# The last product of a two-layer decoder trunk as seven half-size block products, with weight sums made by GpSimd

## The chip, the cores and the metric

The kernel runs on one core of a Trainium2 chip. The metric is the device time of one launch in microseconds (us). The core has TensorE (PE in the profile) for matrix products, VectorE (DVE) and ScalarE (ACT) for elementwise work, GpSimd (POOL) for more of it, and SyncE (SP), which here only starts DMA transfers. The engines run their own instruction lists in order and meet at semaphores.

## The reference, cut to what matters

The stream is 512 tokens by 1024 channels in float32, through two layers. Each layer is a mixer and then a SwiGLU block. The change is in the SwiGLU block of the second layer (l = 1) and in the final norm behind it; D_FF is 2816.

```python
h = rms_norm(x, ffn_norm_w[l])
x = x + (jax.nn.silu(h @ w_gate[l]) * (h @ w_up[l])) @ w_down[l]
...
return rms_norm(x, final_norm_w)
```

The product with `w_down[1]` is the "last product": 512 x 2816 times 2816 x 1024.

## The kernel before

**Precision.** Every large product is made of three TensorE matmuls on rounded float32 (fp32r) operands. A float32 tile W is split into a high part (a ScalarE copy into fp32r, `hi`) and a low part (a VectorE subtraction W - high, `lo`), and the same for the activations; `product` then issues high x high, high x low and low x high.

**The weight stream.** Weights come from HBM in 197 tiles of 128 x 1024 float32 (512 KB) by one DMA each, in SyncE's queue, into `raw`, which has RAW = 2 slots. A slot is loaded again when the split of the tile in it is done. The split goes into `wring`, RING = 4 slots of a high and a low part; ScalarE fills a slot when TensorE has used up the tile four places before (`tile_used`). So TensorE can have at most four split tiles ahead of it. The semaphores of this are `raw_loaded`, `hi_ready`, `lo_ready` and `tile_used`.

**The gate and up products** of layer 2 take 44 tiles, in loops on all engines. Each pair of tiles gives one 128-row block of the activations of the last product, in `AA` (22 blocks, each with a high and a low part of 512 tokens).

**The last product** takes 22 tiles, from T_DN1 on. `token_down(n, u, k)` multiplies token block n (128 of 512 tokens, the stationary operand) and the half u of weight tile k (512 columns, the moving operand) into PSUM bank 2n+u: 4 x 2 x 3 = 24 matmuls for a tile, 528 in all. The last four tiles are run bank by bank, so that the banks close one after another.

**The end.** For each token block VectorE adds the two banks to the residual `resid` (`final_sum`), ScalarE sums squares and takes a root, VectorE makes the reciprocal and the scaled output, and SyncE stores it. The last half block is scaled by ScalarE and stored from ScalarE's queue.

**Order.** All lists are written out by hand; no scheduler moves them. In the last product VectorE has one split per tile and nothing else, and GpSimd has no work at all. GpSimd works in the second layer's mixer alone, beside VectorE and beside the tile splits (`lo`, line 1091); that stage, at 670 to 800 us, is the place of this trace where both run elementwise instructions at once.

## Time and profile before

| | |
|---|---|
| Time before, median of 3 runs | 1249.27 us (1247.49 to 1369.76) |
| The profiled execution | span 1245.8 us from the first to the last instruction; it has no time of its own in the list, and its span is 3.5 us under the median |
| PE, DVE, ACT, POOL busy | 99%, 53%, 39%, 5% of the span |
| Chain that ended last | PE 91%, DVE 4%, ACT 3% |
| Last product on TensorE | 1119.7 to 1239.1 us |
| Granted TensorE clock | 0.999 on the mean |

The profile is of one execution. "Busy" counts the time in which an engine works on an instruction; for TensorE, whose matmuls overlap, it says little on how fast they follow each other, so the prediction counts matmuls in a window instead. The chain that ended last is followed back from the last instruction through whatever each step waited for. The wait rows name the engine and line that waited and what released it.

### The profile page before, as it was taken

The page shows a single profiled execution, that of the slowest core. Times are in us where ns is not written, and L with a number is a line of the kernel's source. Part 1 is how long each engine was busy: PE and PEld are TensorE (multiplying, and loading weights), DVE is VectorE, ACT ScalarE, POOL GpSimd, SP SyncE. Part 2 cuts the span into 40 slices and gives each one's busy share as a digit, 9 for nine tenths or more (in the row PEclk, how much of TensorE's full clock was granted, in tenths as well). Part 3 has the DMA queues.
Part 4 walks back from the last instruction along what each step waited for, and adds up shares of the span by engine and source line. Part 5 has one row for each costly group of instructions (what it writes and reads, how often), then busy time and mean ns, then how long its engine had stood idle before and what let it go on. Part 6 is the DMA issues. An engine that isn't in the chain of part 4 may idle for free.

```text
span 1245.8 us, 16247 instructions
## 1 busy us (share of the span) xinstructions
PE 1232.2 (99%) x5937; PEld 997.3 (80%) x5937; DVE 663.9 (53%) x1075; ACT 486.9 (39%) x802; POOL 65.6 (5%) x161
## 2 busy tenths in 40 slices
PE   9999999999999999999999999999999999999997
PEld 7876657888888888888888788888888888888886
DVE  6787876544444442226677666545644444442224
ACT  6344455433333322124575254544343333322123
POOL 0000000000000000000002814300000000000000
PEclk9999999999999999999999999999999999999999
DMA  7232412323222223222321201012254333223221
GB/s 246 102 112 74 119 38 68 102 102 101 100 91 90 89 101 118 95 90 68 119 85 68 85 35 51 35 51 73 87 145 114 109 101 106 92 101 118 94 93 67
DMA packets 50866, 116.33 MB, mean 93 GB/s; under 512 B 21250, under 2 KB 21506, under 8 KB 50818
## 3 DMA queue, kind: packets, MB, share of 16 engines
q1 hardware_dynamic: 49906, 114.33, 27.8%
q10 hardware_dynamic: 912, 1.35, 0.4%
q8 instruction: 31, 0.51, 0.2%
q14 instruction: 17, 0.14, 0.0%
HBM read 107.11 MB, written 2.10 MB: 88 GB/s over the span
## 4 chain that ended last, share of the span: by engine, by line
PE 91%; DVE 4%; ACT 3%; issue 1%; DMA 0%; ACTq 0%; SPq 0%; DVEq 0%
PE PS L1557 90%; PE PS L1633 0%; DMA raw<-w_stream 0%; DVE cacc L1236 0%; ACTq L793 0%; DVE resid L1532 0%; DVE outT L1548 0%; DVE wring L1091 0%; ACT unread L990 0%; DVE amax L1154 0%; PE PS L1856 0%; ACT wring L668 0%; DVE wbuf L1165 0%; DVE hbuf L1362 0%; ACT pbuf L752 0%
## 5 line engine op out<-in xcount | busy, mean ns | idle before, releaser
L1557 PE MATMUL PS<-HH,wring 128*128 128x512 f32 x3096 | 723.9, 392 | 0.9 <-DVE vd L1489 0.9
L1557 PEld LDWEIGHTS PS<-HH,wring 128*128 128x128 f32 x3096 | 575.4, 188 | 119.0 <-issue 1.3
L1557 PE MATMUL PS<-AA,wring 128*128 128x512 f32 (+1 forms) x792 | 183.3, 391 | 0.4 <-DVE AA L1170 0.3
L1557 PEld LDWEIGHTS PS<-AA,wring 128*128 128x128 f32 x792 | 148.1, 188 | 32.2 <-issue 1.0
L1062 DVE TENSOR_TENSOR ubuf<-PS,rstd 128x512 f32<-128x512 f32 x44 | 30.4, 691 | 191.4 <-PE PS L1557 191.4
L1084 DVE TENSOR_TENSOR wring<-raw,wring 128x1024 fp32r<-128x1024 f32 x36 | 44.1, 1226 | 147.4 <-ACT wring L724 147.4
L1557 PE MATMUL PS<-wring,AA 128*128 128x512 f32 x528 | 119.8, 389 | 0.0
L1557 PEld LDWEIGHTS PS<-wring,AA 128*128 128x128 f32 x528 | 99.1, 188 | 20.6
L1071 DVE TENSOR_TENSOR wring<-raw,wring 128x1024 fp32r<-128x1024 f32 x88 | 107.6, 1222 | 4.1 <-ACT wring L711 3.6
L668 ACT ACTIVATE wring<-raw 128x1024 fp32r<-128x1024 f32 x69 | 72.6, 1057 | 85.1 <-PE PS L1557 65.1
L1091 DVE TENSOR_TENSOR wring<-raw,wring 128x1024 fp32r<-128x1024 f32 x69 | 85.0, 1235 | 34.7 <-ACT wring L668 34.6
L706 ACT ACTIVATE AA<-ubuf 128x512 f32 x44 | 27.9, 633 | 192.1 <-DVE ubuf L1069 192.1
L724 ACT ACTIVATE wring<-raw 128x1024 fp32r<-128x1024 f32 x36 | 38.2, 1061 | 153.3 <-PE PS L1557 147.7
L711 ACT ACTIVATE wring<-raw 128x1024 fp32r<-128x1024 f32 x88 | 92.0, 1046 | 3.6 <-DMA raw<-w_stream 3.6
L700 ACT ACTIVATE gbuf<-gbuf 128x512 f32<-128x512 f32 x44 | 27.8, 632 | 117.1 <-DVE gbuf L1062 117.1
L1062 DVE TENSOR_TENSOR gbuf<-PS,rstd 128x512 f32<-128x512 f32 x44 | 30.4, 690 | 37.3 <-PE PS L1557 37.1
L1557 PE MATMUL PS<-wring,HH 128*128 128x512 f32 x192 | 45.8, 393 | 0.7 <-ACT wring L738 0.7
L1557 PEld LDWEIGHTS PS<-wring,HH 128*128 128x128 f32 x192 | 35.5, 188 | 8.5 <-issue 1.3
L752 ACT ACTIVATE pbuf<-PS,amax 128x128 f32<-128x128 f32 (+3 forms) x32 | 16.6, 524 | 47.6 <-DVE amax L1154 47.6
L1069 DVE TENSOR_TENSOR ubuf<-gbuf,ubuf 128x512 f32<-128x512 f32 x44 | 30.4, 692 | 5.8
L612 POOL MEMSET cin<- 128x3 f32 x1 | 0.1, 102 | 587.5 <-DVE xT L1052 587.5
L672 ACT ACTIVATE HH<-xT,vec 128x512 fp32r<-128x512 f32 x32 | 22.9, 716 | 20.0 <-DVE xT L1052 16.8
(282 smaller groups left out, 1043.4 us busy)
## 6 DMA issues: line engine op xcount, KB each, us to landing
raw<-w_stream SPq DMA_DIRECT2D x193, 512.0 KB, 3.3
reps<-ub SPq DMA_DIRECT2D x32, 66.5 KB, 2.1
resid<-turned SPq DMA_DIRECT2D x16, 128.0 KB, 4.9
out_t<-outT SPq DMA_DIRECT2D x3, 512.0 KB, 2.6
reps_b<-ub SPq DMA_DIRECT2D x16, 66.5 KB, 2.1
reps<-ub ACTq DMA_DIRECT2D x16, 66.5 KB, 2.4
xT<-x_t SPq DMA_DIRECT2D x4, 256.0 KB, 5.3
raw<-w_stream SPq DMA_DIRECT2D x4, 256.0 KB, 5.8
```

The costliest lines, as they stand in the source:

```text
L668: nc.scalar.activation(wring[:, t % RING, 0], raw_tile(t), ACT.Copy).then_inc(hi_ready[t % RING], 1)
L672: nc.scalar.activation(HH[:, n, 0], xT[:, n], ACT.Copy, scale=vcol(V_NORM + KD * s + n)).then_inc(feed_hi, 1)
L700: nc.scalar.activation(gbuf[:, c], gbuf[:, c], ACT.Silu).then_inc(sem("gate_silu"), 1)
L706: nc.scalar.activation(AA[:, bass.ds(r * 2 + c, 1), 0].rearrange("p a b -> p (a b)"), ubuf[:, c], ACT.Copy).then_inc(sem("ffn_hi"), 1)
L711: nc.scalar.activation(wring[:, t % RING, 0], raw[:, t % RAW], ACT.Copy).then_inc(hi_ready[t % RING], 1)
L724: nc.scalar.activation(wring[:, t % RING, 0], raw[:, t % RAW], ACT.Copy).then_inc(hi_ready[t % RING], 1)
L1062: V.tensor_tensor(buf[:, c], PS[:, 2 * c + u], rstd[:], ALU.mult).then_inc(evacuated, 1)
L1069: V.tensor_tensor(ubuf[:, c], gbuf[:, c], ubuf[:, c], ALU.mult).then_inc(sem("ffn_mul"), 1)
L1071: V.tensor_tensor(wring[:, t % RING, 1], raw[:, t % RAW], wring[:, t % RING, 0].bitcast(f32), ALU.subtract).then_inc(lo_ready[t % RING], 1)
L1084: V.tensor_tensor(wring[:, t % RING, 1], raw[:, t % RAW], wring[:, t % RING, 0].bitcast(f32), ALU.subtract).then_inc(lo_ready[t % RING], 1)
L1091: V.tensor_tensor(wring[:, t % RING, 1], raw_tile(t), wring[:, t % RING, 0].bitcast(f32), ALU.subtract).then_inc(lo_ready[t % RING], 1)
L1557: return nc.tensor.matmul(out, lhsT, rhs, start=start, stop=stop)
```

## The change

The last product is cut into a 2 x 2 scheme: tokens in halves (0 to 255 and 256 to 511), the 22 row blocks of the weights by parity (11 even, 11 odd), the columns in halves of 512. With A11, A12, A21, A22 for the activations (token half, parity) and B11, B12, B21, B22 for the weights (parity, column half), seven products of half the size in each of the three directions take the place of eight. The weights of the last product come from their own tensor `w_last`, block by block, in pieces of two rows of 128 x 512 (PIECES = 6 for one block: five of 1024 columns and one of 512). The code's products run in this order:

| product (pieces g) | activations | weights |
|---|---|---|
| P_12 (0 to 5) | A11 | B12, from the stream |
| P_11 (6 to 11) | A21 - A22 | B11, loaded into `kept` |
| P_22 (12 to 17) | A12 | B22, from the stream |
| P_21 (18 to 23) | A22 | B11 + B21, in `kept` |
| P_SUM (24 to 29) | A11 - A21 + A22 | B11 + B21 + B22, in `kept` |
| P_ALL (30 to 35) | A21 - A11 | B11 + B21 + B22 + B12, in `kept` |
| P_LAST (36 to 41) | A12 - A11 + A21 - A22 | B22, loaded into `kept` anew, + B21 |

- GpSimd adds an addend to each piece of `kept` in place, 24 additions (`add_to_kept`). The addends are loaded by SyncE into two slots (`addends`), and a slot is loaded again when its addition is done. An addition also waits until VectorE has split the piece's earlier value.
- Each of the 42 pieces is split as before by ScalarE (`last_hi`) and VectorE (`last_lo`), four pieces ahead of TensorE at most.
- The sums of activations are made by VectorE: two subtractions in each round of the gate/up loop, and pairs of instructions on 128 x 512 with a split behind them between the pieces (`last_product`), the splits' high parts by ScalarE.
- Two PSUM banks for each product; P_22, P_21 and P_LAST add onto banks that hold an earlier product. Behind a product, VectorE adds its banks to `resid` and to two snapshots (`after_product`).
- The loads of `kept` begin when the gate and up products are over, since they lie where HH was.
- The output order becomes token blocks 2, 3, 0, 1; the squares of half of the outputs are summed earlier. Elsewhere some semaphores are merged.

```diff
-N_TILES = T_DN1 + KF
+N_TILES = T_DN1
+HALF = KF // 2
+PIECES = (HALF + 1) // 2
+PRODUCTS = 7
...
+B11, B12, B21, B22 = (0, 0), (0, 1), (1, 0), (1, 1)
+P_12, P_11, P_22, P_21, P_SUM, P_ALL, P_LAST = range(PRODUCTS)
+OUT_ORDER = (2, 3, 0, 1)
+BANK_12, BANK_21, BANK_SUM, BANK_22 = 4, 6, 0, 2
+PRODUCT_BANK = (BANK_12, BANK_21, BANK_12, BANK_21, BANK_SUM, BANK_22, BANK_SUM)
+RING_PRODUCTS = (P_12, P_22)
+ADDED = (P_21, P_SUM, P_ALL, P_LAST)
+ADDENDS = 2
+ADDED_PARTS = {P_21: (B21, P_11), P_SUM: (B22, P_21), P_ALL: (B12, P_SUM), P_LAST: (B21, P_ALL)}
...
+    pfull, q = at("pfull", [HALF, 2 * P], f32, SCRATCH + 128)
+    assert q <= base
+    kept, q = at("kept", [HALF, S], f32, at_H)
+    addends, q = at("addends", [ADDENDS, TILE], f32, q)
+    assert q <= at_H + 32768
...
+        def ring_load(g, part):
+            v = ring_use(g)
+            before = ring_before(v - RAW)
+            sp.wait_ge(hi_ready[before % RING], slot_round(before))
+            sp.wait_ge(lo_ready[before % RING], slot_round(before))
+            n = len(piece_rows(g % PIECES)) * S
+            sp.dma_start(raw[:, v % RAW, 0:n], last_d[part][:, columns_of(g % PIECES)]).then_inc(raw_loaded[v % RAW], 16)
...
+        for i in range(PIECES):
+            ring_load(P_12 * PIECES + i, B12)
+        sp.wait_ge(tile_used, T_DN1)
+        for i in range(PIECES):
+            sp.dma_start(kept_tile(i), last_d[B11][:, columns_of(i)]).then_inc(kept_loaded[i], 16)
+        def load_addend(a, i):
+            d = ADDED.index(a) * PIECES + i
+            if d >= ADDENDS:
+                sp.wait_ge(added, d - ADDENDS + 1)
+            n = len(piece_rows(i)) * S
+            sp.dma_start(addends[:, d % ADDENDS, 0:n], last_d[ADDED_PARTS[a][0]][:, columns_of(i)]).then_inc(addend_loaded[d % ADDENDS], 16)
...
+        for i in range(PIECES):
+            if i == RAW:
+                for k in range(PIECES):
+                    load_addend(P_21, k)
+            ring_load(P_22 * PIECES + i, B22)
+        for a in (P_SUM, P_ALL):
+            for i in range(PIECES):
+                load_addend(a, i)
+        for i in range(PIECES):
+            free = last_tile(P_ALL * PIECES + i)
+            sp.wait_ge(lo_ready[free % RING], slot_round(free))
+            sp.dma_start(kept_tile(i), last_d[B22][:, columns_of(i)]).then_inc(kept_loaded[i], 16)
+            load_addend(P_LAST, i)
...
+        def add_to_kept(a, i):
+            d = ADDED.index(a) * PIECES + i
+            free = last_tile(ADDED_PARTS[a][1] * PIECES + i)
+            pool.wait_ge(lo_ready[free % RING], slot_round(free))
+            if a == P_LAST:
+                pool.wait_ge(kept_loaded[i], 48)
+            elif a > P_21:
+                pool.wait_ge(added, added_count(ADDED[ADDED.index(a) - 1], i))
+            pool.wait_ge(addend_loaded[d % ADDENDS], 16 * (d // ADDENDS + 1))
+            n = len(piece_rows(i)) * S
+            nc.gpsimd.tensor_tensor(kept_tile(i), kept_tile(i), addends[:, d % ADDENDS, 0:n], ALU.add).then_inc(added, 1)
...
+        for a in ADDED:
+            for i in range(PIECES):
+                add_to_kept(a, i)
...
+        def last_hi(g):
+            product, i = divmod(g, PIECES)
+            t = last_tile(g)
+            n = len(piece_rows(i)) * S
+            if product in RING_PRODUCTS:
+                v = ring_use(g)
+                act.wait_ge(raw_loaded[v % RAW], raw_count(v))
+                src = raw[:, v % RAW, 0:n]
+            else:
+                if product == P_11:
+                    act.wait_ge(kept_loaded[i], 32)
+                else:
+                    act.wait_ge(added, added_count(product, i))
+                src = kept_tile(i)
+            act.wait_ge(tile_used, t - RING + 1)
+            nc.scalar.activation(wring[:, t % RING, 0, 0:n], src, ACT.Copy).then_inc(hi_ready[t % RING], 1)
...
+                    V.tensor_tensor(ubuf[:, c], gbuf[:, c], ubuf[:, c], ALU.mult).then_inc(sem("ffn_mul"), 1)
+                    if c:
+                        dve.wait_ge(sem("ffn_mul"), r * 3 + (KF + 2))
+                        V.tensor_tensor(ubuf[:, 0, 2 * P:S], ubuf[:, 0, 2 * P:S], ubuf[:, 1, 2 * P:S], ALU.subtract).then_inc(sem("ffn_mul"), 1)
+                    loop_lo(r, tg + RING + 2 * c)
+                    if c:
+                        dve.wait_ge(sem("ffn_mul"), r * 3 + (KF + 3))
+                        V.tensor_tensor(pfull[:, bass.ds(r, 1)].rearrange("p a b -> p (a b)"), ubuf[:, 0, 0:2 * P], ubuf[:, 0, 2 * P:S],
+                                        ALU.subtract).then_inc(sem("lhs_made"), 1)
...
+        def last_lo(g):
+            product, i = divmod(g, PIECES)
+            t = last_tile(g)
+            n = len(piece_rows(i)) * S
+            src = raw[:, ring_use(g) % RAW, 0:n] if product in RING_PRODUCTS else kept_tile(i)
+            dve.wait_ge(hi_ready[t % RING], slot_round(t))
+            V.tensor_tensor(wring[:, t % RING, 1, 0:n], src, wring[:, t % RING, 0, 0:n].bitcast(f32), ALU.subtract).then_inc(lo_ready[t % RING], 1)
...
+        def after_product(product):
+            banks = [PS[:, PRODUCT_BANK[product] + b] for b in range(2)]
+            if product == P_11:
+                dve.wait_ge(sem("last_act"), 2)
+            for b in range(2):
+                product_done(dve, product, b)
+                if product == P_11:
+                    V.tensor_tensor(snap(b), banks[b], snap(b), ALU.add).then_inc(sem("last_sums"), 1)
+                elif product == P_22:
+                    dve.wait_ge(sem("last_sums"), sums_made(P_11, b))
+                    add_residual(b, 1, banks[b], ALU.add).then_inc(sem("final_x"), 1)
+                    link(add_residual(b, 0, snap(b), ALU.add))
+                    add_residual(b, 0, banks[b], ALU.subtract).then_inc(sem("last_sums"), 1)
...
+        def last_product():
+            dve.wait_ge(sem("lhs_made"), HALF)
+            dve.wait_ge(sem("resid_loaded"), 16 * 16)
+            for g in range(RING, PRODUCTS * PIECES):
+                last_lo(g)
+                if 5 <= g < 11:
+                    i = g - 5
+                    dve.wait_ge(sem("ffn_lo"), 2 * KF)
+                    link(V.tensor_tensor(scratch(i), second_more(i, 0).bitcast(f32), full_sum(i), ALU.subtract))
+                    V.tensor_tensor(scratch(i), scratch(i), second_more(i, 1).bitcast(f32), ALU.add).then_inc(sem("lhs_made"), 1)
+                if 6 <= g < 12:
+                    i = g - 6
+                    dve.wait_ge(sem("ffn_hi"), 2 * KF + i + 1)
+                    V.tensor_tensor(first_rows(i, 1), scratch(i), first_rows(i, 0).bitcast(f32), ALU.subtract).then_inc(sem("ffn_lo"), 1)
+                elif 12 <= g < 18:
+                    i = g - 12
+                    dve.wait_ge(sem("ffn_hi"), 2 * KF + PIECES + i + 1)
+                    V.tensor_tensor(first_diff(i, 1), full_sum(i), first_diff(i, 0).bitcast(f32), ALU.subtract).then_inc(sem("ffn_lo"), 1)
+                if 17 <= g < 29 and g % 2 == 1:
+                    i = (g - 17) // 2
+                    link(V.tensor_tensor(scratch(i), second_rows(i, 0).bitcast(f32), full_sum(i), ALU.subtract))
+                    V.tensor_tensor(scratch(i), scratch(i), second_rows(i, 1).bitcast(f32), ALU.add).then_inc(sem("lhs_made"), 1)
+                elif 18 <= g < 30:
+                    i = (g - 18) // 2
+                    dve.wait_ge(sem("ffn_hi"), 2 * KF + 2 * PIECES + i + 1)
+                    V.tensor_tensor(second_rows(i, 1), scratch(i), second_rows(i, 0).bitcast(f32), ALU.subtract).then_inc(sem("ffn_lo"), 1)
+                if g % PIECES == 4 and g // PIECES >= 2:
+                    after_product(g // PIECES - 1)
...
-        def token_down(n, u, k):
-            return product(PS[:, 2 * n + u], (AA[:, k, 0, blk(n)], AA[:, k, 1, blk(n)]), wpair((T_DN1 + k) % RING, slice(u * S, (u + 1) * S)),
-                           k == 0, k == KF - 1)
-        pe.wait_ge(norm_rstd, 4)
...
+        def left(product, r, b):
+            some = slice(b * P, (b + 1) * P)
+            more = slice((2 + b) * P, (3 + b) * P)
+            of = {P_12: (0, some), P_11: (0, more), P_22: (1, some), P_21: (1, more), P_SUM: (0, more), P_ALL: (0, some), P_LAST: (1, some)}[product]
+            return pairs_of[:, r, of[0], 0, of[1]], pairs_of[:, r, of[0], 1, of[1]]
...
+        def piece(a, i, b):
+            adds = a in (P_22, P_21, P_LAST)
+            t = last_tile(a * PIECES + i)
+            for m, r in enumerate(piece_rows(i)):
+                last = product(PS[:, PRODUCT_BANK[a] + b], left(a, r, b), wpair(t % RING, slice(m * S, (m + 1) * S)),
+                               r == 0 and not adds, r == HALF - 1, adds)
+            return last
+        for a in range(PRODUCTS):
+            bank_ready(a)
+            for i in range(PIECES if a < P_LAST else PIECES - RING):
+                arrived(last_tile(a * PIECES + i))
+                left_ready(a, i)
+                last = piece(a, i, 0)
+                if i == PIECES - 1:
+                    last.then_inc(last_mm, 1)
+                piece(a, i, 1).then_inc(tile_used, 1)
```

How the lists read before and after, at three places. The names: `wring` is the ring of split pieces, `raw` the slots of loads, `kept` and `addends` as above, `pfull` holds A11 - A21 + A22, `gbuf` and `ubuf` are scratch, `ssq` and `rstd` are the two snapshots.

VectorE in the last product, before: tiles 4 places ahead of TensorE, then the end.

```order
L1084 TENSOR_TENSOR wring<-raw,wring 128x1024 [waits hi_ready0]
L1084 TENSOR_TENSOR wring<-raw,wring 128x1024 [waits hi_ready1]
L1084 TENSOR_TENSOR wring<-raw,wring 128x1024 [waits hi_ready2]
L1080 REGISTER_ALU
L1080 COMPARE_AND_BRANCH
L1091 TENSOR_TENSOR wring<-raw,wring 128x1024 [waits hi_ready3]
L1091 TENSOR_TENSOR wring<-raw,wring 128x1024 [waits hi_ready0]
L1532 TENSOR_TENSOR resid<-resid,PS 128x512 [waits token_down,final_loaded,resid_loaded]
L1536 TENSOR_SCALAR nst<-ost 128x1 [waits final_sq]
L1532 TENSOR_TENSOR resid<-resid,PS 128x512 [waits token_down]
```

VectorE after, from the first split of product P_21 (g = 18) on.

```order
L1342 TENSOR_TENSOR wring<-kept,wring 128x1024 [waits hi_ready1]
L1399 TENSOR_TENSOR AA<-gbuf,AA 128x2x256 [waits ffn_hi]
L1342 TENSOR_TENSOR wring<-kept,wring 128x1024 [waits hi_ready2]
L1394 TENSOR_TENSOR gbuf<-AA,pfull 128x512
L1395 TENSOR_TENSOR gbuf<-gbuf,AA 128x512 [waits dve_chain]
L1342 TENSOR_TENSOR wring<-kept,wring 128x1024 [waits hi_ready3]
L1399 TENSOR_TENSOR AA<-gbuf,AA 128x2x256 [waits ffn_hi]
L1342 TENSOR_TENSOR wring<-kept,wring 128x1024 [waits hi_ready0]
L1394 TENSOR_TENSOR ubuf<-AA,pfull 128x512
L1395 TENSOR_TENSOR ubuf<-ubuf,AA 128x512 [waits dve_chain]
L1342 TENSOR_TENSOR wring<-kept,wring 128x1024 [waits hi_ready1]
L1399 TENSOR_TENSOR AA<-ubuf,AA 128x2x256 [waits ffn_hi]
```

Between two splits there now stand one or two instructions more for the activations' sums, whose inputs are all in SBUF as the splits' are; a split of `kept` waits for ScalarE, which waits for GpSimd.

GpSimd's list, before: its last rows, at the end of the mixer of layer 2.

```order
L650 TENSOR_TENSOR G_122<-G_122 128x4x2 [waits gdn1_pool]
L648 TENSOR_TENSOR G_122<-G_123,G_122 128x4 [waits gdn1_pool]
L650 TENSOR_TENSOR G_122<-G_122 128x4 [waits gdn1_pool]
L653 TENSOR_TENSOR G_123<-G_122,consts 128x512 [waits gdn1_pool]
L2107 UNCONDITIONAL_BRANCH
```

GpSimd after: from the fourth of the 24 additions on, which stand behind the same L653 row (now L788).

```order
L803 TENSOR_TENSOR kept<-kept,addends 128x1024 [waits addend_loaded1,lo_ready0]
L803 TENSOR_TENSOR kept<-kept,addends 128x1024 [waits addend_loaded0,lo_ready1]
L803 TENSOR_TENSOR kept<-kept,addends 128x512 [waits addend_loaded1,lo_ready2]
L803 TENSOR_TENSOR kept<-kept,addends 128x1024 [waits addend_loaded0,added,lo_ready1]
L803 TENSOR_TENSOR kept<-kept,addends 128x1024 [waits addend_loaded1,added,lo_ready2]
L803 TENSOR_TENSOR kept<-kept,addends 128x1024 [waits addend_loaded0,added,lo_ready3]
```

A list that had ended goes on with additions, each of which waits for a load and for a split by VectorE, and from the seventh on for an earlier addition.

TensorE at the end, before: the last full tile, and the four that are run bank by bank.

```order
L1557 MATMUL PS<-wring,AA 128x512 [waits ffn_lo,lo_ready0,hi_ready0]
L1557 MATMUL PS<-wring,AA 128x512 x23
L1557 MATMUL PS<-wring,AA 128x512 [waits lo_ready1,hi_ready1,ffn_lo]
L1557 MATMUL PS<-wring,AA 128x512 x5
L1557 MATMUL PS<-wring,AA 128x512 [waits lo_ready2,hi_ready2]
L1557 MATMUL PS<-wring,AA 128x512 x5
L1557 MATMUL PS<-wring,AA 128x512 [waits lo_ready3,hi_ready3]
L1557 MATMUL PS<-wring,AA 128x512 x5
L1557 MATMUL PS<-wring,AA 128x512 [waits lo_ready0,hi_ready0]
L1557 MATMUL PS<-wring,AA 128x512 x77
```

TensorE after: the start of P_LAST and the end.

```order
L1876 MATMUL PS<-wring,AA 128x512 [waits lo_ready3,ffn_lo,hi_ready3,last_sums]
L1876 MATMUL PS<-wring,AA 128x512 x11
L1876 MATMUL PS<-wring,AA 128x512 [waits ffn_lo,lo_ready0,hi_ready0]
L1876 MATMUL PS<-wring,AA 128x512 x11
L1876 MATMUL PS<-wring,AA 128x512 [waits ffn_lo,lo_ready1,hi_ready1]
L1876 MATMUL PS<-wring,AA 128x512 x5
L1876 MATMUL PS<-wring,AA 128x512 [waits ffn_lo,lo_ready2,hi_ready2]
L1876 MATMUL PS<-wring,AA 128x512 x5
L1876 MATMUL PS<-wring,AA 128x512 [waits ffn_lo,lo_ready3,hi_ready3]
L1876 MATMUL PS<-wring,AA 128x512 x5
L1876 MATMUL PS<-wring,AA 128x512 [waits ffn_lo,lo_ready0,hi_ready0]
L1876 MATMUL PS<-wring,AA 128x512 x23
```

A piece of 1024 columns is now 12 matmuls where a tile was 24, and every piece waits anew for its split; the last two banks close 21 matmuls apart (the 24 of the last row less 3 that still belong to the first bank), where two banks before were 12 apart.

## Rows read from the trace of the kernel before

**Rows 1.** The page: its first line, busy engines, chain that ended last.

```profile
span 1245.8 us, 16247 instructions
PE 1232.2 (99%) x5937; PEld 997.3 (80%) x5937; DVE 663.9 (53%) x1075; ACT 486.9 (39%) x802; POOL 65.6 (5%) x161
...
PE 91%; DVE 4%; ACT 3%; issue 1%; DMA 0%; ACTq 0%; SPq 0%; DVEq 0%
```

**Rows 2.** Stretches: times, busy and instructions of PE, PEld, DVE, ACT, POOL; clock, DMA.

```profile
1120.00:1160.00 40.00, 40.00 (x178) 33.12 (x177) 12.34 (x12) 9.01 (x9) 0.00 (x0) 1.00 0.30 106
1119.70:1239.10 119.40, 119.35 (x527) 98.50 (x525) 35.58 (x42) 27.50 (x37) 0.00 (x0) 1.00 0.25 89
```

**Rows 3.** Waits from 1120 us on: who for whom, total, times, longest.

```profile
DVE wring L1084 <- ACT wring L724: 65.3, 16, 4.2
ACT wring L724 <- PE PS L1557: 65.2, 15, 4.4
...
SPq L580 <- DVE wring L1084: 78.6, 16, 5.0
```

**Rows 4.** Groups of the page: shapes, count, busy us, mean ns, idle before.

```profile
L1084 DVE TENSOR_TENSOR wring<-raw,wring 128x1024 fp32r<-128x1024 f32 x36 | 44.1, 1226 | 147.4 <-ACT wring L724 147.4
...
L724 ACT ACTIVATE wring<-raw 128x1024 fp32r<-128x1024 f32 x36 | 38.2, 1061 | 153.3 <-PE PS L1557 147.7
...
L1069 DVE TENSOR_TENSOR ubuf<-gbuf,ubuf 128x512 f32<-128x512 f32 x44 | 30.4, 692 | 5.8
```

**Rows 5.** Timeline, GpSimd with little beside it: start us, us, what.

```profile
776.66 1.29 POOL L633 TENSOR_TENSOR G<-G,consts 128x512 f32<-128x512 f32 x1 [8.21 <-DVE kT L1421]
...
778.03 0.74 POOL L635 TENSOR_TENSOR G<-G 128x256 f32<-128x256 f32 x1
...
778.84 0.47 POOL L637 TENSOR_TENSOR G<-G 128x128 f32<-128x128 f32 x1
```

**Rows 6.** Timeline, VectorE and GpSimd at once.

```profile
675.75 1.55 POOL L627 TENSOR_TENSOR vtok<-vtok,beta 128x512 f32<-128x512 f32 x1
676.33 0.68 DVE L1407 TENSOR_TENSOR G<-kT,PS 128x512 f32<-128x512 f32 x1
...
686.52 1.25 DVE L1091 TENSOR_TENSOR wring<-raw,wring 128x1024 fp32r<-128x1024 f32 x1
686.68 2.25 POOL L633 TENSOR_TENSOR G<-G,consts 128x512 f32<-128x512 f32 x1
689.01 0.74 POOL L635 TENSOR_TENSOR G<-G 128x256 f32<-128x256 f32 x1
689.05 1.78 DVE L1091 TENSOR_TENSOR wring<-raw,wring 128x1024 fp32r<-128x1024 f32 x1 [1.28 <-ACT wring L668]
...
701.05 1.23 DVE L1091 TENSOR_TENSOR wring<-raw,wring 128x1024 fp32r<-128x1024 f32 x1 [0.46 <-ACT wring L668]
701.26 1.09 POOL L650 TENSOR_TENSOR G<-G 128x16 f32<-128x16 f32 x1
702.44 0.21 POOL L648 TENSOR_TENSOR G<-G 128x12 f32<-128x12 f32 x1
```

**Rows 7.** DMA: issues from 1120 us (KB, median us to landing); stretch at the start.

```profile
raw<-w_stream SPq DMA_DIRECT2D x18, 512.0 KB, 3.2
...
12.00:16.00 4.00, 4.00 (x19) 3.33 (x18) 3.90 (x6) 3.84 (x7) 0.00 (x0) 1.00 1.03 410
```

**Rows 8.** Timeline as the last product begins.

```profile
1119.21 8.10 PE L1557 MATMUL PS<-wring,AA 128*128 128x512 f32 x35
1119.41 0.69 DVE L1062 TENSOR_TENSOR ubuf<-PS,rstd 128x512 f32<-128x512 f32 x1 [4.75 <-PE PS L1557]
...
1122.68 1.23 DVE L1071 TENSOR_TENSOR wring<-raw,wring 128x1024 fp32r<-128x1024 f32 x1
```

**Rows 9.** One-microsecond stretches behind the last matmul, columns as in rows 2.

```profile
1243.00:1244.00 1.00, 0.00 (x0) 0.00 (x0) 0.00 (x0) 0.00 (x0) 0.00 (x0) 0.72 0.45 168
1244.00:1245.00 1.00, 0.00 (x0) 0.00 (x0) 0.00 (x0) 0.00 (x0) 0.00 (x0) 0.50 0.95 356
```

379 lines of the change are left out of this document (246 added, 133 removed).

## The prediction

> **What bounds the kernel now.** I read the page first: TensorE is busy 99% of the span and holds 91% of the chain that ended last [rows 1]. Busy time of overlapping matmuls doesn't give their pace, so the next view is the stretches: 40 us inside the last product hold 178 matmuls, 0.2247 us each, and the whole product, 1119.7 to 1239.1, has 527 recorded of its 528 [rows 2]; 528 x 0.2247 = 118.6 us. The waits then show who is late: VectorE waits for ScalarE, ScalarE for TensorE, SyncE for VectorE's split, each some 65 to 79 us of these 119 [rows 3]. So TensorE alone sets the pace, and VectorE with 36 us and ScalarE with 27 us of work [rows 2] have much to spare. GpSimd does nothing there. The question is whether that stays so when TensorE's work shrinks and everybody else's grows.
>
> **TensorE's part, certain.** Seven products x 11 row blocks x 2 banks x 3 = 462 matmuls of the same shape, 66 fewer: 66 x 0.2247 = 14.8 us less. A product is 66 x 0.2247 = 14.8 us, a full piece (12 matmuls) 2.70 us, all seven 103.8 us.
>
> **What the others get.** Durations: a split of 1024 columns 1.23 us on VectorE and 1.06 on ScalarE; a VectorE instruction on 512 columns with both inputs in SBUF 0.69 [rows 4], which gives 0.42 for 256. GpSimd's additions on 1024 columns are in no row. Two-input instructions with little beside them took 0.47 for 128 columns, 0.74 for 256 and 1.29 for 512 [rows 5]: a straight line of 2.14 ns a column over 0.19 us, so 2.38 us for 1024 and 1.29 for the half piece. The 512-column row has a broadcast second input, and the line is stretched to twice its length, so I keep 2.2 and 2.6 as ends and take 2.38, since three rows lie on the line. A product's six additions take 5 x 2.38 + 1.29 = 13.2 us. By itself that fits under 14.8.
>
> The Trainium skill (GPSIMD Engine Reference, § 3.1 Elementwise — side-by-side cycle accounting) gives 4497 ns for an addition of 2048 columns; an estimate from it would be 2.25 us for 1024 and take about 2 us off the forecast. No row here has that width, and I go by the line.
>
> **The term that decides: VectorE and GpSimd don't overlap.** The timeline shows it [rows 6], in both directions. GpSimd's L633, 1.29 alone, started at 686.68 during a split and took 2.25: the split ended at 687.77, and the addition 1.16 later. The split that started at 689.05 while GpSimd's L635 ran until 689.75 took 1.78 instead of 1.23, ending 1.08 after it. A GpSimd instruction of 16 columns, 0.21 like its neighbour, took 1.09 beside a split. But VectorE's L1407, with one input in PSUM, took its usual 0.68 within GpSimd's 1.55. So VectorE instructions with two SBUF inputs and GpSimd's additions run one after the other, each for its duration less some 0.13 us of start: 1.10, 0.56 and 0.29 us for VectorE's three sizes, 2.26 and 1.17 for GpSimd's. I call this held time.
>
> The Trainium skill (SBUF — State Buffer, § Who interferes with whom) states this as an exclusive lock, for VectorE instructions with two SBUF inputs against GpSimd reads; it is the rule that speaks against this change. The trace agrees, with the rows just read. If it held only for some forms, the first rival below would be the result.
>
> All splits and all sums of activations have two SBUF inputs. Held time by product, from the list of the change (the splits of a product are always 5 x 1.10 + 0.56 = 6.1):
> - P_11: splits 6.1, sums 13 x 0.56 + 3 x 0.29 = 8.2, together 14.2; the first six additions, 5 x 2.26 + 1.17 = 12.5, fall here too.
> - P_22: splits 6.1, sums 7 x 0.56 + 0.29 = 4.2; no additions, since the next need the splits of P_21.
> - P_21: splits 6.1, sums 9 x 0.56 = 5.0, two snapshots onto `resid` 1.1, additions 12.5: 24.7.
> - P_SUM: splits 6.1, sums 4 x 0.56 + 4 x 0.29 = 3.4, snapshots 1.1, additions 12.5: 23.1.
> - P_ALL and P_LAST: splits 6.1 each, one set of additions, 12.5.
>
> TensorE offers 14.8 for each. Now in time, from TensorE's first matmul of the last product as zero.
>
> *P_12 and P_11.* The end of the gate/up loop keeps VectorE busy for 4 us past zero [rows 8], and the two new subtractions of 256 columns add 0.9: the last split of the loop ends near 5. Then SyncE loads piece 5 and the pieces of `kept`. A 512 KB transfer lands in 3.2 us, of which some 1.3 is transfer when several stand in line (410 GB/s) [rows 7]. `kept` 0 lands near 9.6, and its split starts near 11, when TensorE wants it at 14.8: no loss yet, but most of the lead of four pieces is gone. The addends stand behind eight transfers and GpSimd starts near 20. From 11 on the port is held 14.2 + 12.5 and 1.1 for the first split of P_22: P_22 can't start before 39, against 29.7. That is 9 late at least; I take 10.
> *P_22.* Its held time fits, but with two slots a pair of pieces takes a load, a copy and a split, 3.2 + 1.06 + 1.23 = 5.5, against TensorE's 5.4, so no lead is won back, and the first splits come with waits: 2 late, 0 at least.
> *P_21.* 24.7 - 14.8 = 9.9 late at least. Every split waits for ScalarE's copy (1.06), which VectorE can't fill, and the four PSUM instructions of `after_product` (4 x 0.68) leave the port idle behind the addition that runs with them: 2 more, 12.
> *P_SUM.* 23.1 - 14.8 = 8.3 at least, 10.5 likely, for the same reason.
> *P_ALL and P_LAST.* Held time over both is 12.2 + 12.5 = 24.7, under 29.6; P_ALL finds its sums made. P_LAST's need a new load of `kept` first: 1.5 late.
>
> Sum: 10 + 2 + 12 + 10.5 + 0 + 1.5 = 36 us late, less 14.8: **21 us slower**. At least: 9 + 0 + 9.9 + 8.3 = 27 late, +12. At most within this mechanism: no saving of the 0.13 us at the hand-overs, some 60 instructions in the three bound stretches, 8 us more, +29.
>
> **Edits at nothing.** The loop's new waits and subtractions cost VectorE 0.9 us per round of 21.6 us (96 matmuls), in which it works some 11; cover is the ring. The banks' waits (`last_act`, `last_sums`) are met a product ahead. The end: the last chain (residual, square, root, reciprocal, scaling, store) has the same instructions, and the other last bank closes 21 matmuls, 4.7 us, ahead, which covers its block's 3.5; within 0.5 us. More traffic, some 22 MB in 140 us, is 160 GB/s against the 410 of [rows 7]. The merged semaphores lie beside matmuls.
>
> **Time.** The profiled execution has a span of 1245.8 us, 3.5 under the median; the change is taken against both alike. 1249.3 + 21 = about **1271 us**. A measurement of this kernel can tell about 2%, 25 us, from no change.
>
> **Rivals.**
> *No block for these forms* (GpSimd's addition in place with plain inputs, VectorE's splits of `kept`). Then all fits under TensorE: 103.8, plus about 5: GpSimd begins at 20, SyncE's third piece of P_22 stands behind four of its additions and arrives near 36 where 35 is wanted, and the splits of P_21 and P_SUM follow with 1 to 2 us each. 118.6 - 108.8 = 10 less, 1240 us. This is the case on the faster side, though within 2%: 14.8 is all there is to win. For it: nothing but that no row shows a 1024-column addition. Against it: [rows 6]. Chance 0.14, with partial blocking in it (1235 to 1255).
> *TensorE's clock falls in its new gaps.* After the last matmul the granted clock was 0.72 in the fifth microsecond and 0.50 in the sixth [rows 9], 1.2 GHz. I expect gaps of 1 to 4 us between pieces, the longest at the ends of P_11, P_21 and P_SUM, some 45% of the time in P_21. At half clock a product takes 29.7, over the 26.8 and 25.3 that the port allows: 2.9 + 4.4, and 2 or so after P_11: 1280 us. It decides for slower by over 2% (above 1274.3). Against it: gaps between pieces are shorter than the idle time that the row shows. Chance 0.17 (1278 to 1290).
> The Trainium skill (TensorE: Matmul & The Clock Gate, § HAM oscillation — how this bites in real kernels) says that idle gaps between bursts of matmuls return the array to half clock; by it this rival would be the result, and [rows 9] agree only on the fall after the end.
> *The change doesn't do what it says:* excluded for the matmuls, which the order shows.
> *Worse than all this* (transfers late as well, GpSimd over 2.6 us): 0.06, above 1290.
>
> **The numbers.** Forecast 0.63, over 1261 to 1279, a quarter of it above 1274.3. Range 1250 to 1288: it leaves out most of the no-block case, the end of the clock case and the worst, 0.2. Slower by over 2%: 0.17 + 0.06 + 0.16 = 0.39; within 2%: 0.60; faster by over 2%: 0.01, since 14.8 us is 1.2%.
>
> **What will show it.** Additions of 1024 columns at 2.4 us where VectorE is idle and 3 to 3.5 beside it; splits of 1.2 us stretched to 2 to 3.5. TensorE dense until the end of P_11, then a matmul share near 55% in P_21 and P_SUM, waiting for splits; dense again in P_ALL. TensorE's last product 140 us long. If additions and splits overlap at their own durations, the step on held time is wrong; if `kept` or addends land late and GpSimd waits for DMA, the one on transfers is.

## The result and the profile after

The changed kernel takes 1272.49 us (median of 4 runs, 1270.81 to 1273.22), the kernel before 1248.42 us on the same chip. The ratio is 1.0196, with a 95% interval of 1.0182 to 1.0210: 24 us slower, where 21 to 22 were forecast (1271). The 1248.42 is the median of four runs, one of which, 1369.76 us, the ratio leaves out; the median of the other three is 1247.57 us.

The page of the profiled execution after: first line, busy engines, the 40 slices of three engines and of the clock, and the chain that ended last. It answers to [rows 1].

```profile
span 1271.1 us, 16397 instructions
...
PE 1229.4 (97%) x5871; PEld 989.1 (78%) x5871; DVE 762.8 (60%) x1172; ACT 515.9 (41%) x844; POOL 126.5 (10%) x185
...
PE   9999999999999999999999999999999999997677
...
DVE  6787876544444442227777566446654454578997
...
POOL 0000000000000000000006535000000000004544
PEclk9999999999999999999999999999999999998999
...
PE 84%; DVE 9%; ACT 3%; issue 2%; DMA 2%; ACTq 0%; POOL 0%; SPq 0%; DVEq 0%; POOLq 0%
```

TensorE has 66 matmuls fewer and 2.8 us less busy time, yet the span is 25.3 us longer: in the last four slices, where POOL shows 4 and 5, those of PE fall from 9 to 6 and 7. On the chain, PE fell from 91% to 84% and DVE rose from 4% to 9%.

TensorE's timeline in the last product (start, us, what; in brackets the idle time ahead and who ended it):

```profile
1120.96 15.35 PE L1876 MATMUL PS<-wring,AA 128*128 128x512 f32 x67
...
1152.71 4.32 PE L1876 MATMUL PS<-wring,AA 128*128 128x512 f32 x12 [5.75 <-DVE wring L1342]
1159.07 14.29 PE L1876 MATMUL PS<-wring,AA 128*128 128x512 f32 x54 [2.04 <-DVE wring L1342]
...
1179.10 2.97 PE L1876 MATMUL PS<-wring,AA 128*128 128x512 f32 x12 [1.06 <-DVE wring L1342]
1183.05 3.01 PE L1876 MATMUL PS<-wring,AA 128*128 128x512 f32 x12 [0.97 <-DVE wring L1342]
1187.59 3.01 PE L1876 MATMUL PS<-wring,AA 128*128 128x512 f32 x12 [1.54 <-DVE wring L1342]
...
1202.76 2.41 PE L1876 MATMUL PS<-wring,AA 128*128 128x512 f32 x6 [3.66 <-DVE wring L1342]
1206.29 7.51 PE L1876 MATMUL PS<-wring,AA 128*128 128x512 f32 x24 [1.12 <-DVE wring L1342]
...
1231.52 23.50 PE L1876 MATMUL PS<-wring,AA 128*128 128x512 f32 x102 [0.95 <-issue]
...
1257.43 5.71 PE L1876 MATMUL PS<-wring,AA 128*128 128x512 f32 x24 [0.17 <-issue]
```

The last product runs from 1120.96 to 1263.14, 142.2 us, against 119.84 before (1119.21 to 1239.05; it starts in [rows 8]). It is dense for P_12 and the first four of P_11's six pieces, waits 5.75 and 2.04 us ahead of the last two, has a gap ahead of nearly every piece of P_21 and P_SUM, and is dense again from P_ALL (1231.52) on. "Issue" in brackets does not mean that nothing was waited for: the weight load, which stands ahead of the matmul, took the wait for the split.

The stretches P_11, P_21 and P_SUM, columns as in [rows 2]:

```profile
1135.90:1161.60 25.70, 17.91 (x67) 13.83 (x66) 25.56 (x20) 9.58 (x14) 15.38 (x6) 0.88 0.46 163
1179.10:1206.30 27.20, 17.41 (x67) 12.32 (x67) 27.03 (x22) 8.72 (x14) 15.72 (x7) 0.95 0.33 93
1206.30:1231.50 25.20, 18.08 (x66) 13.34 (x67) 25.06 (x21) 9.75 (x15) 14.58 (x6) 0.92 0.29 88
```

VectorE, 36 us busy in the old last product [rows 2], is busy in 99% of each of these. GpSimd has spare time in all three. What VectorE does with its time is in the groups of the stretch 1119 to 1263 us (shapes, count, busy us, mean ns, idle before; the first row is GpSimd's):

```profile
L803 POOL TENSOR_TENSOR kept<-kept,addends 128x1024 f32<-128x1024 f32 x20 | 54.5, 2726 | 387.9 <-DMA addends<-w_last 354.9 <-DVE wring L1342 33.0
L1342 DVE TENSOR_TENSOR wring<-kept,wring 128x1024 fp32r<-128x1024 f32 x25 | 49.6, 1993 | 3.2 <-ACT wring L907 3.1
...
L1346 DVE TENSOR_TENSOR resid<-resid,PS 128x512 f32<-128x512 f32 x13 | 8.5, 680 | 0.1
...
L1382 DVE TENSOR_TENSOR gbuf<-AA,pfull 128x256 f32<-128x256 f32 x1 | 2.6, 2577 | 0.0
```

Splits of 1024 columns take 1993 ns on the mean, against 1226 in [rows 4]; one subtraction of 256 columns takes 2577 ns, where the prediction has 0.42 us for that width. The form with one input in PSUM (`resid<-resid,PS`) takes 680 ns, as before. And so it looks in time, in P_21:

```profile
1179.04 2.78 POOL L803 TENSOR_TENSOR kept<-kept,addends 128x1024 f32<-128x1024 f32 x1 [18.64 <-DVE wring L1342]
...
1179.48 3.42 DVE L1342 TENSOR_TENSOR wring<-kept,wring 128x1024 fp32r<-128x1024 f32 x1
...
1182.82 0.68 DVE L1394 TENSOR_TENSOR gbuf<-AA,pfull 128x512 f32<-128x512 f32 x1
1182.98 2.79 POOL L803 TENSOR_TENSOR kept<-kept,addends 128x1024 f32<-128x1024 f32 x1 [1.16 <-DVE wring L1342]
...
1183.53 2.78 DVE L1395 TENSOR_TENSOR gbuf<-gbuf,AA 128x512 f32<-128x512 f32 x1
```

The split begins 0.44 us after the addition and ends 1.08 after it (1182.90 against 1181.82). The next addition begins during VectorE's L1394 and ends 2.27 after it; L1395, behind it, ends 0.54 after that. These are the turns of the prediction, 2.26, 1.10 and 0.56 us: each instruction starts its own work when the other engine's has ended.

**The sum, read off the starts.** P_12, P_11, P_22, P_21, P_SUM and P_ALL start at 0, 15.0, 40.6, 58.1, 85.3 and 110.6 us after TensorE's first matmul, and P_LAST ends at 142.2.

| stretch | late, predicted | late, measured |
|---|---|---|
| to the start of P_22 | 10 | 10.7 |
| P_22 | 2 | 2.5 |
| P_21 | 12 | 12.2 |
| P_SUM | 10.5 | 10.3 |
| P_ALL and P_LAST | 1.5 | 1.7 |
| matmuls saved | -14.8 | -15.0 |
| last product | +21 | +22.3 |

"Late" is what lies over 14.96 us a product (66 x 0.2267: the 119.45 us from the first to the last matmul's start before, divided by 527 steps). The span's other 3 us: the last product starts 1.75 us later, and what follows the last matmul takes 8.0 instead of 6.75 us.

### The profile page after: what moved, and what is told of

It reads as the page before. It is cut to its first block, busy times and chain, and to the rows that moved or that the text cites. A ratio compares the mean times of both kernels' runs of the same rounds, so it can differ in the third digit from the quotient of the medians.

```text
span 1271.1 us, 16397 instructions
## 1 busy us (share of the span) xinstructions
PE 1229.4 (97%) x5871; PEld 989.1 (78%) x5871; DVE 762.8 (60%) x1172; ACT 515.9 (41%) x844; POOL 126.5 (10%) x185
## 4 chain that ended last, share of the span: by engine, by line
PE 84%; DVE 9%; ACT 3%; issue 2%; DMA 2%; ACTq 0%; POOL 0%; SPq 0%; DVEq 0%; POOLq 0%
PE PS L1876 83%; DVE wring L1342 2%; DMA raw<-w_last 1%; DVE resid L1346 1%; DVE gbuf L1382 1%; PE PS L1952 1%; DVE AA L1387 0%; DVE cacc L1550 0%; POOL kept L803 0%; ACTq L1015 0%; DVE gbuf L1383 0%; ACT wring L907 0%; DVE ubuf L1395 0%; DVE wring L1405 0%; DMA raw<-w_stream 0%
## 5 line engine op out<-in xcount | busy, mean ns | idle before, releaser
L1278 DVE TENSOR_TENSOR wring<-raw,wring 128x1024 fp32r<-128x1024 f32 x108 | 131.0, 1221 | 84.7 <-ACT wring L848 84.5
L848 ACT ACTIVATE wring<-raw 128x1024 fp32r<-128x1024 f32 x108 | 113.3, 1049 | 115.9 <-PE PS L1876 107.3
L1876 PE MATMUL PS<-wring,AA 128*128 128x512 f32 x462 | 115.3, 407 | 26.9 <-DVE wring L1342 19.0
L1876 PEld LDWEIGHTS PS<-wring,AA 128*128 128x128 f32 x462 | 89.0, 196 | 53.0 <-issue 34.9
L820 ACT ACTIVATE wring<-raw 128x1024 fp32r<-128x1024 f32 x67 | 70.5, 1057 | 77.0 <-PE PS L1876 56.8
L803 POOL TENSOR_TENSOR kept<-kept,addends 128x1024 f32<-128x1024 f32 (+1 forms) x24 | 61.2, 2553 | 396.9 <-DMA addends<-w_last 354.9
L1405 DVE TENSOR_TENSOR wring<-raw,wring 128x1024 fp32r<-128x1024 f32 x67 | 82.5, 1234 | 25.9 <-ACT wring L820 25.8
L1342 DVE TENSOR_TENSOR wring<-kept,wring 128x1024 fp32r<-128x1024 f32 (+1 forms) x30 | 54.0, 1808 | 3.2 <-ACT wring L907 3.1
L907 ACT ACTIVATE wring<-kept 128x1024 fp32r<-128x1024 f32 (+1 forms) x30 | 28.8, 978 | 16.9 <-PE PS L1876 8.4
```

The costliest lines, as they stand in the source:

```text
L803: nc.gpsimd.tensor_tensor(kept_tile(i), kept_tile(i), addends[:, d % ADDENDS, 0:n], ALU.add).then_inc(added, 1)
L820: nc.scalar.activation(wring[:, t % RING, 0], raw_tile(t), ACT.Copy).then_inc(hi_ready[t % RING], 1)
L848: nc.scalar.activation(wring[:, t % RING, 0], raw[:, t % RAW], ACT.Copy).then_inc(hi_ready[t % RING], 1)
L907: nc.scalar.activation(wring[:, t % RING, 0, 0:n], src, ACT.Copy).then_inc(hi_ready[t % RING], 1)
L1278: V.tensor_tensor(wring[:, t % RING, 1], raw[:, t % RAW], wring[:, t % RING, 0].bitcast(f32), ALU.subtract).then_inc(lo_ready[t % RING], 1)
L1342: V.tensor_tensor(wring[:, t % RING, 1, 0:n], src, wring[:, t % RING, 0, 0:n].bitcast(f32), ALU.subtract).then_inc(lo_ready[t % RING], 1)
```

## The experiments

Theory 1 is the prediction's: GpSimd's additions and VectorE's instructions with two inputs in SBUF take turns, and VectorE, which feeds TensorE, has no time for it in P_11, P_21 and P_SUM. Rival 2: not the turns, but the chain load, addition, split and the late addends. Rival 3: TensorE's clock. All edits are to the changed kernel, unless said otherwise, and are compared with its 1272.49 us above; "of before" is the kernel before beside the same runs (1247.69 to 1247.82 us). The first four (8 columns, memsets, half the columns, less work for VectorE) leave out part of the sums and are there for the time alone. "Last product" is its length on TensorE.

### Additions on 8 columns

```diff
-            nc.gpsimd.tensor_tensor(kept_tile(i), kept_tile(i), addends[:, d % ADDENDS, 0:n], ALU.add).then_inc(added, 1)
+            nc.gpsimd.tensor_tensor(kept_tile(i)[:, 0:8], kept_tile(i)[:, 0:8], addends[:, d % ADDENDS, 0:8], ALU.add).then_inc(added, 1)
```

> The changed kernel with each of the 24 weight additions of GpSimd on 8 of its 1024 (512) columns; every wait, load and semaphore stays, so the sums of the weights are left out. Theory 1 (GpSimd's additions and VectorE's subtractions with two inputs in SBUF hold each other up, and that is the whole loss): with the additions near 0.2 us nothing is left to block, the last product takes 105 us of matmuls and the first waits of the loads, 107 to 112 us, and the time is 1238 to 1243 us. Rival 2 (the loss is the chain: addends load only when an addition is done, and a piece's split waits for its sum): at least half of the 22 us stays, 1255 to 1270 us. Rival 3 (half clock in the gaps carries the loss): since the gaps go with the additions, it gives the same as theory 1 here and is told apart by the run with filled gaps.

1234.96 us, 0.9894 of before (0.9874 to 0.9914): 37.5 us less than the changed kernel, and 13 of the 15 us under the kernel before that 66 matmuls fewer allow. That is 3 us below the 1238 to 1243 expected. With every load, wait and semaphore in place the last product took 108.2 us, within the 107 to 112 expected; what follows the last matmul took 5.7 us instead of the changed kernel's 8.0, and the last product began at 1119.36 instead of 1120.96. Its timeline on TensorE:

```profile
1119.36 35.52 PE L1876 MATMUL PS<-wring,AA 128*128 128x512 f32 x156
1155.19 5.70 PE L1876 MATMUL PS<-wring,AA 128*128 128x512 f32 x24 [0.30 <-DVE wring L1342]
1161.21 4.33 PE L1876 MATMUL PS<-wring,AA 128*128 128x512 f32 x18 [0.32 <-DVE wring L1342]
1166.41 15.24 PE L1876 MATMUL PS<-wring,AA 128*128 128x512 f32 x66 [0.87 <-DVE wring L1342]
1182.46 45.12 PE L1876 MATMUL PS<-wring,AA 128*128 128x512 f32 x198 [0.81 <-DVE wring L1342]
```

Over the matmuls' 105 us (462 x 0.2267, and the last one's length) some 3 us are left: the 0.30 and 0.32 us stand in P_22, whose pieces are loaded, the 0.87 and 0.81 us at the starts of P_21 and P_SUM, where VectorE had worked without a pause since 1159.84. The rest of the loss hangs on the additions' width. That excludes the loads, but a tiny addition also answers some 2 us sooner, so it doesn't yet tell turns from latency.

### GpSimd as busy, but only writing

```diff
-            nc.gpsimd.tensor_tensor(kept_tile(i), kept_tile(i), addends[:, d % ADDENDS, 0:n], ALU.add).then_inc(added, 1)
+            nc.gpsimd.memset(addends[:, d % ADDENDS, 0:n], 0.001).then_inc(sem("warm_zero"), 1)
+            pool.wait_ge(sem("warm_zero"), d + 2)
+            nc.gpsimd.memset(kept_tile(i), 0.001).then_inc(added, 1)
```

> The changed kernel with two memsets (one of the addend slot, one of the kept piece) in place of each addition, so the sums of the weights are left out: GpSimd is busy about as long as with the addition (some 2.1 against 2.4 us for 1024 columns) and answers as late, but reads no SBUF. Theory 1, in the form that it is GpSimd's reads that stand against VectorE's: VectorE's splits of kept pieces stay near 1.3 us against 1.99 after, and the time is 1238 to 1246 us. Rival 2 (it is GpSimd's late answer, however it comes about): 1258 to 1270 us with splits near 1.3 us. A third way, writes contend as reads do: splits near 2 us and 1262 to 1272 us.

1239.54 us (two runs, 1237.49 and 1241.60; the profile is of the latter), 0.9931 of before (0.9908 to 0.9953). The last product took 111.7 us. The groups of this run:

```profile
L1344 DVE TENSOR_TENSOR wring<-kept,wring 128x1024 fp32r<-128x1024 f32 x25 | 30.5, 1222 | 11.2 <-ACT wring L909 11.0
...
L805 POOL MEMSET kept<- 128x1024 f32 x20 | 19.1, 957 | 1.1
L803 POOL MEMSET addends<- 128x1024 f32 x20 | 19.1, 956 | 383.3 <-DMA addends<-w_last 369.4 <-DVE wring L1344 13.8
```

A pair of memsets takes 2.0 us from start to end where an addition alone takes 2.4 (2.7 on the mean in the changed kernel), and the splits are at their own 1222 ns. Rival 2 expected 1258 or more. An answer nearly as late as the addition's costs 4.6 us over the run with 8 columns, for an answer 1.4 us later (there the additions took 0.57 us on the mean). At that price the 0.4 to 0.8 us by which the pair is still shorter than an addition are worth 1 to 3 us (an estimate). The other 30 of the 33 us up to the changed kernel are the reads' turns, which is theory 1.

The Trainium skill (SBUF — State Buffer, § Who interferes with whom) names a GpSimd instruction that reads SBUF as the other side, and not one that only writes it. The trace agrees: 1222 ns beside memsets, 1993 beside additions.

### Additions on half the columns

```diff
-            nc.gpsimd.tensor_tensor(kept_tile(i), kept_tile(i), addends[:, d % ADDENDS, 0:n], ALU.add).then_inc(added, 1)
+            nc.gpsimd.tensor_tensor(kept_tile(i)[:, 0:n // 2], kept_tile(i)[:, 0:n // 2], addends[:, d % ADDENDS, 0:n // 2], ALU.add).then_inc(added, 1)
```

> The changed kernel with each GpSimd addition on half of its columns (512 of 1024, 256 of 512), so the sums of the weights are left out in the other half. Theory 1: an addition then holds VectorE up for 1.17 instead of 2.26 us, additions and splits of a piece fit into the 2.72 us of its matmuls, and only the pieces at the end of P_11 and in P_21, where VectorE has its own sums too, are late: 5 to 14 us remain over the 105 of the matmuls, and the time is 1243 to 1254 us. In proportion to the width (rival: each us of GpSimd costs the same): 1254 us, half way between 1235 and 1272.5.

1250.03 us (1248.37 to 1253.16; the profile is of the slowest run), within theory 1's 1243 to 1254. The last product took 122.7 us: the first half of the width costs 14.5 us in it (from 108.2) and the second 19.5. A straight line between the two ends would give 125.2. That the second half costs more fits theory 1, where additions cost nothing until VectorE's spare time is used up. But the distance, 2.5 us, is small, and the run tells little between the two forms.

### Less work for VectorE, additions whole

```diff
-link(V.tensor_tensor(scratch(i), second_more(i, 0).bitcast(f32), full_sum(i), ALU.subtract))
-V.tensor_tensor(scratch(i), scratch(i), second_more(i, 1).bitcast(f32), ALU.add)
+link(V.tensor_tensor(scratch(i)[:, :, 0:8], second_more(i, 0)[:, :, 0:8].bitcast(f32), full_sum(i)[:, :, 0:8], ALU.subtract))
+V.tensor_tensor(scratch(i)[:, :, 0:8], scratch(i)[:, :, 0:8], second_more(i, 1)[:, :, 0:8].bitcast(f32), ALU.add)
```

and the same for `second_rows`.

> The changed kernel with the 22 VectorE subtractions and additions that make the left factors of P_SUM and P_LAST from the halves (two per piece, in the loops of 5 <= g < 11 and 17 <= g < 29) on 8 columns of each row; the weight additions stay whole, so the products of the two left sums are left out. Theory 1: what GpSimd blocks is VectorE's queue, so work taken off VectorE (some 13 us of duration, and the turns that it would wait for) gives back its share: 8 to 16 us less in the last product, 1256 to 1265 us. If the additions on GpSimd alone paced the pieces, at one per 2.4 to 2.8 us: no more than 3 us, 1269 to 1273 us.

1260.46 us (1259.93 and 1260.99), where theory 1 had 1256 to 1265 and a pace set by GpSimd 1269 or more. The last product took 130.8 us, 11.3 less than in the changed kernel. Three of the groups:

```profile
L803 POOL TENSOR_TENSOR kept<-kept,addends 128x1024 f32<-128x1024 f32 x20 | 54.4, 2727 | 376.6 <-DMA addends<-w_last 353.2 <-DVE wring L1342 23.4
...
L1395 DVE TENSOR_TENSOR gbuf<-gbuf,AA 128x8 f32<-128x8 f32 x1 | 2.4, 2378 | 0.0
...
L1394 DVE TENSOR_TENSOR gbuf<-AA,pfull 128x16 f32<-128x16 f32 x3 | 0.5, 163 | 0.0
```

The 24 instructions (the expectation says 22; it is four for each of six pieces) come to 20 x 0.69 + 4 x 0.42 = 15.5 us by their own lengths at full width and to some 24 x 0.17 = 4.1 now, 11.4 less. They were not that short in the trace: six of them still waited out an addition, as the one on 8 columns that took 2378 ns, and all 24 were busy 16.1 us, against 31.1 in the changed kernel. An addition costs its turn whatever VectorE has next, but the work taken off VectorE came back whole in the last product (11.4 and 11.3 us), while GpSimd's additions took as long as ever. So the limit is VectorE's queue, with the additions in it as if they were its own, and not the pace of GpSimd.

### The additions on VectorE

```diff
+        def add_to_kept(a, i):
+            d = ADDED.index(a) * PIECES + i
+            if a == P_LAST:
+                dve.wait_ge(kept_loaded[i], 48)
+            dve.wait_ge(addend_loaded[d % ADDENDS], 16 * (d // ADDENDS + 1))
+            n = len(piece_rows(i)) * S
+            V.tensor_tensor(kept_tile(i), kept_tile(i), addends[:, d % ADDENDS, 0:n], ALU.add).then_inc(added, 1)
...
                 last_lo(g)
+                for ahead in (4, 3):
+                    if P_21 * PIECES <= g + ahead and (ahead == 3) == (g + ahead >= P_LAST * PIECES) and g + ahead < PRODUCTS * PIECES:
+                        add_to_kept(*divmod(g + ahead, PIECES))
...
         for i in range(PIECES):
-            if i == RAW:
-                for k in range(PIECES):
-                    load_addend(P_21, k)
             ring_load(P_22 * PIECES + i, B22)
+            for k in ((), (0, 1), (), (2,), (3,), (4, 5))[i]:
+                load_addend(P_21, k)
```

> The same 24 additions, each by VectorE four pieces ahead of its use (three for the last product), GpSimd idle, and the P_21 addends loaded between the P_22 pieces on SyncE's queue. VectorE's busy time rises by 24 x 1.15 = 28 us, and none of its instructions is stretched. Theory 1: TensorE waits some 15 us for VectorE in P_22 to P_SUM, where additions, splits and activation sums come to more than the product's 15 us; the last product takes 118 to 125 us, and the time is 1247 to 1256 us, against 1272.5 with GpSimd and 1248.4 before. If the additions cost the same wherever they run (chain or loads): 1265 to 1275 us.

1254.33 us (1253.68 to 1255.51), 1.0051 of before (1.0035 to 1.0068), within the 1247 to 1256 expected. The stretch from the first wait in P_22 to P_ALL, columns as in [rows 2]:

```profile
1163.00:1210.00 47.00, 40.23 (x144) 30.30 (x144) 46.65 (x60) 18.78 (x29) 0.00 (x0) 0.85 0.46 135
```

and the group of the additions:

```profile
L1362 DVE TENSOR_TENSOR kept<-kept,addends 128x1024 f32<-128x1024 f32 x20 | 24.4, 1220 | 3.1 <-DMA addends<-w_last 3.1
```

An addition on VectorE takes 1.22 us of VectorE; on GpSimd it takes 2.26 us of VectorE. Taking all of them back is 18 us faster. But VectorE is still full here (46.65 of 47 us), the last product takes 124.5 us, and the change still doesn't pay. The clock is 0.85 in this stretch; what part of the 20 us over the matmuls' 105 is the clock's wasn't taken apart.

### The gaps filled, to keep the clock

```diff
+                spin({10: 38, 11: 12, 23: 24, 29: 22}.get(a * PIECES + i, 0))
                 arrived(last_tile(a * PIECES + i))
...
+        def spin(n):
+            if n:
+                pe.wait_ge(evacuated, E_GU1 + 2 * KF)
+            for _ in range(n):
+                mm(PS[:, BANK_22, 0:2 * P], pairs_of[:, 0, 1, 0, 2 * P:3 * P], pairs_of[:, 0, 1, 0, 2 * P:S])
```

> The changed kernel with 38, 12, 24 and 22 extra matmuls of 256 columns into a free PSUM bank ahead of the pieces 10, 11, 23 and 29, where TensorE idles 5.75, 2.04, 3.66 and 3.39 us, to keep its clock up. Rival 3 (the clock carries the loss): the pieces behind go at full clock (4.32 us of twelve matmuls back to 2.7, 7.51 us of 24 back to 5.5), and the time falls by 4 to 8 us, to 1264 to 1268 us. Theory 1: the pieces go faster but then wait for the same splits, and the time falls by 0 to 3 us, 1269.5 to 1273 us.

1272.67 us (1271.94 to 1273.64), against 1272.49 for the changed kernel: no change, where the rival had 1264 to 1268. The clock had fallen in the changed kernel. Two stretches of it, columns as in [rows 2], the granted clock third from the right:

```profile
1152.00:1156.00 4.00, 3.29 (x9) 2.67 (x10) 3.96 (x4) 0.44 (x2) 3.61 (x2) 0.57 0.50 138
...
1203.00:1211.00 8.00, 6.88 (x19) 4.98 (x19) 7.93 (x7) 2.53 (x3) 5.07 (x3) 0.57 0.34 91
```

and with the gaps filled:

```profile
1151.60:1154.60 3.00, 2.96 (x14) 2.50 (x15) 2.96 (x3) 0.09 (x1) 2.54 (x2) 1.00 0.47 158
...
1203.00:1211.00 8.00, 6.07 (x20) 4.81 (x20) 7.96 (x6) 2.53 (x3) 5.07 (x3) 0.79 0.44 131
```

The piece behind the longest gap, 4.32 us for twelve matmuls after, took 2.99 here at full clock. It gave nothing back, since the next piece still waited 1.97 us for its split: P_ALL began 110.45 us after the first matmul, against 110.56 in the changed kernel. The second place was mended only in part (0.79, 24 matmuls in 7.32 us, against 7.51). At full clock 24 matmuls take 5.71, as at 1257.43 in the changed kernel, so 1.8 us are at stake there. The next piece waited 0.80 us for its split after them all the same, and VectorE was busy 7.93 of those 8.00 us, which speaks for this fall being free too. The run shows it of the first fall only.

Behind P_ALL this run had a wait of 2.38 us in P_LAST that the changed kernel did not have; GpSimd had waited 2.92 and 1.38 us there for addends to land. Its last product was 145.2 us long for that, its start 1.2 us earlier and its end 1.4 us shorter than in the changed kernel. So the equal times alone would not show that the clock is free; the equal starts of P_ALL do.

### The kernel before, with additions beside it

```diff
+        pool.wait_ge(tile_used, T_DN1)
+        for m in range(2):
+            nc.gpsimd.memset(unused[:, m], 0.001).then_inc(sem("warm_zero"), 1)
+            pool.wait_ge(sem("warm_zero"), m + 2)
+        for k in range(KF - RING):
+            pool.wait_ge(tile_used, T_DN1 + max(k - 1, 0))
+            nc.gpsimd.tensor_tensor(unused[:, 0], unused[:, 0], unused[:, 1], ALU.add).then_inc(sem("warm_zero"), 1)
+            pool.wait_ge(sem("warm_zero"), k + 4)
```

> The kernel before, with 18 additions of 1024 columns on GpSimd, kept = kept + addend on unused SBUF that nothing else reads, one released by each finished weight tile of the last product. Theory 1, in the form that the blocking costs time only where VectorE has none to spare: VectorE is busy 1.23 us of each 5.4 us there, its splits beside an addition stretch from 1.23 to up to 3.4 us, TensorE waits for none, and the time stays at 1247 to 1250 us. If additions on GpSimd slow the kernel by themselves (SBUF traffic, TensorE's reads): 18 x some tenths of a us, 1252 us or more.

1247.70 us, 1.0001 of before (0.9990 to 1.0011), within the 1247 to 1250 expected. One round in the timeline:

```profile
1141.38 2.40 POOL L664 TENSOR_TENSOR unused<-unused 128x1024 f32<-128x1024 f32 x1 [3.04 <-PE PS L1567]
1142.37 2.50 DVE L1094 TENSOR_TENSOR wring<-raw,wring 128x1024 fp32r<-128x1024 f32 x1 [2.94 <-ACT wring L734]
```

and the groups of TensorE and of the splits:

```profile
L1567 PE MATMUL PS<-wring,AA 128*128 128x512 f32 x528 | 119.8, 389 | 0.0
...
L1094 DVE TENSOR_TENSOR wring<-raw,wring 128x1024 fp32r<-128x1024 f32 x16 | 40.8, 2550 | 41.1 <-ACT wring L734 41.1
```

Here nothing depends on the additions. The splits take 2550 ns on the mean, twice their length, and the one shown ends 1.09 us after the addition (1144.87 against 1143.78), as the pair at 689 us in [rows 6] does (1.08); the splits take 21 us more in all, and TensorE waits for none of it. The turns are there without any chain between the two engines, and cost nothing where VectorE has time.

### The additions by DMA

```diff
-            pool.wait_ge(addend_loaded[d % ADDENDS], 16 * (d // ADDENDS + 1))
-            n = len(piece_rows(i)) * S
-            nc.gpsimd.tensor_tensor(kept_tile(i), kept_tile(i), addends[:, d % ADDENDS, 0:n], ALU.add).then_inc(added, 1)
+            nc.gpsimd.dma_start(kept_tile(i), last_d[ADDED_PARTS[a][0]][:, columns_of(i)], accum_op=ALU.add).then_inc(accumulated[d % 3], 16)
```

with a wait for the transfer three places before, and ScalarE's copies waiting for `accumulated`; the loads of addends are gone.

> The whole product, with each weight sum made by the DMA: an accumulating transfer from DRAM onto the kept piece, issued on GpSimd's queue in place of the addition; no addend slots, no addition on any engine. Theory 1: nothing holds up VectorE, and the time is that of the run with tiny additions, 1234 to 1242 us, below the kernel before. Against it: an accumulating transfer reads and writes SBUF beside the DRAM and takes longer than the 3.6 us of a plain one; at 6 pieces of lead (15 us of a product) it is hidden up to some 10 us. If its transfer takes longer than that, or its descriptors cost GpSimd and the queues over 2.7 us a piece: 1250 us or more.

1243.41 us (1242.20 to 1245.04), 0.9965 of before (0.9951 to 0.9979). The splits took 1221 ns. The issues, from the DMA view (KB, median us to landing):

```profile
kept<-w_last POOLq DMA_DIRECT2D x20, 512.0 KB, 7.6
raw<-w_last SPq DMA_DIRECT2D x10, 512.0 KB, 4.0
kept<-w_last SPq DMA_DIRECT2D x10, 512.0 KB, 6.7
```

and the two longest waits in TensorE's timeline:

```profile
1156.50 5.72 PE L1868 MATMUL PS<-wring,AA 128*128 128x512 f32 x24 [2.23 <-DVE wring L1334]
...
1215.83 10.04 PE L1868 MATMUL PS<-wring,AA 128*128 128x512 f32 x36 [1.95 <-DVE wring L1334]
```

It missed its expectation (1234 to 1242) by 1.4 us, and the last product took 114.9 us. An accumulating transfer takes 7.6 us from issue to landing, a plain one of the same size 4.0 or 6.7, some of it standing in line with others. Ahead of the first wait ScalarE had waited 6.02 us for a plain load, whose slot comes free late; ahead of the second, 8.16 us for a piece of P_LAST, which is loaded and then added to. One more kernel gave both places more lead: pieces 0 and 1 of P_22 load into the two free addend slots, and P_LAST adds B21 where P_22 left pieces 0, 1, 4 and 5 of B22.

```diff
-            nc.gpsimd.dma_start(kept_tile(i), last_d[ADDED_PARTS[a][0]][:, columns_of(i)], accum_op=ALU.add)
+            nc.gpsimd.dma_start(last_source(a, i), last_d[ADDED_PARTS[a][0]][:, columns_of(i)], accum_op=ALU.add)
...
+        for i in range(2):
+            sp.dma_start(addends[:, i], last_d[B22][:, columns_of(i)]).then_inc(first_loaded[i], 16)
+        for i in range(2, PIECES):
+            ring_load(P_22 * PIECES + i, B22)
```

> The run with DMA additions (1243.4 us), with its two longest waits of TensorE taken away: 2.23 us ahead of the third piece of P_22, whose load waits for a slot, and 1.95 us ahead of P_LAST, whose pieces are loaded and then added to in turn. The pieces 0 and 1 of P_22 load into the two free addend slots as soon as the last product begins, and P_LAST adds B21 onto the pieces 0, 1, 4 and 5 of B22 where P_22 left them; only the pieces 2 and 3 are loaded again. Theory 1 with the DMA's lead as the only rest: 3 to 6 us less (the waits and the half clock behind the second, 36 matmuls in 10.04 us against 8.2), 1237 to 1241 us. If the waits are those of the accumulating transfers in general (7.6 us from issue to landing), they turn up at the next piece: 1242 to 1245 us.

1239.59 us (1238.77 to 1240.24), 0.9933 of before (0.9919 to 0.9947), within the 1237 to 1241 expected: the fastest kernel that computes the whole result, 8 us under the one before and 33 under the changed one. The last product took 110.6 us. The first wait is gone; in place of the second there are two, 1.45 and 1.39 us, further into P_LAST:

```profile
1119.29 45.06 PE L1878 MATMUL PS<-wring,AA 128*128 128x512 f32 x198
1165.10 15.25 PE L1878 MATMUL PS<-wring,AA 128*128 128x512 f32 x66 [0.75 <-DVE wring L1344]
...
1218.21 1.63 PE L1878 MATMUL PS<-wring,AA 128*128 128x512 f32 x6 [1.45 <-issue]
1221.22 8.62 PE L1878 MATMUL PS<-wring,AA 128*128 128x512 f32 x36 [1.39 <-issue]
```

## Why the prediction was right

**The term that decides** held. VectorE's two-input instructions and GpSimd's additions take turns, with the turn lengths that were read off [rows 6]. In P_21 two pieces have two additions, two splits and three sums: 2 x 2.26 + 2 x 1.10 + 3 x 0.56 = 8.4 us; TensorE's pieces there start 8.49 apart (1179.10 to 1187.59). The runs with 8 columns, with memsets and with less VectorE work each take away one side. What they leave to other causes (the loads, VectorE's own work and the late answer) is 7 us together: 111.7 us with memsets, less the matmuls' 105.

**The addition's length**, 2.38 off a line through three narrower rows, was 2.37 to 2.42 where VectorE left it alone (1149.10: 2.37, and 2.40 in the old kernel with additions). The estimate of 2.25 from the Trainium skill's table (GPSIMD Engine Reference, § 3.1 Elementwise — side-by-side cycle accounting) was 6% short of that. Beside VectorE the additions took 2.73 on the mean and 2.79 in P_21, less than the 3 to 3.5 named as a sign: there an addition stood behind the end of an earlier VectorE instruction only, and it was VectorE's own that were stretched.

**The lateness by product** was right to 0.7 us each, as the table shows. The places were right too: P_11's end, all of P_21 and P_SUM, nearly dense from P_ALL on (its longest gap there is 0.62 us). GpSimd's first addition came 21.1 us after TensorE's first matmul, where 20 stood.

**Sizes that were off, all small.** The pace, 0.2247 us, was read from a count in a window that takes in matmuls cut by both of its edges; from first to last it is 0.2267, 1 us more for 528. "The end ... within 0.5 us" was 1.2 us: VectorE's last residual add began 2.3 us after the last matmul, since `after_product(P_ALL)` and the scaled outputs of two blocks stood ahead of it; before, it began 1.2 us after. The later start of the last product, 1.75 us, was in no term. It goes with a granted clock of 0.83 at 800 to 810 us, far ahead of the change:

```profile
800.00:810.00 10.00, 10.00 (x69) 9.56 (x68) 3.51 (x6) 4.99 (x9) 0.00 (x0) 0.83 0.14 40
```

The profiled runs with half-width additions and with memsets have the same 0.83 and start at 1120.68 and 1120.31; the other six of the changed kernel's variants start at 1118.76 to 1119.78, with 1.00. What sets it off stays open.

**Luck in the total.** The forecast of 1271 is 1.5 us from the measured 1272.49, nearer than its terms were. The base of 1249.3 us lies 1.7 above the 1247.57 us of the three runs that agree, and the change itself was 24.9 us by these medians and 25.3 by the spans, some 4 over the 21 of the sum: the last product's 1.3, the start's 1.75 and the end's 1.2.

**The rivals.** *No block for these forms* (1240) didn't come; the run with memsets, 1239.5 us, shows what it would have been. *The clock falls in the gaps* came in its first half: the granted clock was at its lower level, 1.2 GHz, for some 3 us behind the gap of 5.75 us, for 3 more behind the 2.04 us that followed it, and for 6 to 7 behind the one of 3.66. It stayed at 1.00 behind the 3.39 us ahead of P_SUM's last piece. So the prediction's argument against it, that these gaps are shorter than the idle time of [rows 9], did not hold. But the fall did not get its price of 9 us. The step of that rival that failed is half clock for a whole product: P_21 has 0.95 with a gap of 1 to 1.5 us ahead of nearly every piece, P_SUM 0.92, and the piece that ran slow behind the longest gap was waited out by the next split anyway. What the fall at the start of P_SUM cost, 1.8 us at most by the 24 matmuls there, stays open; if it cost anything, P_SUM's 10.3 us of lateness hold it.

## What to carry to other kernels

Work given to GpSimd is not off VectorE's back if it reads SBUF while VectorE's instructions read two inputs there: count it in VectorE's time, at GpSimd's duration, and see whether the sum still fits under the matmuls. Where it does, as in the kernel before with additions beside it, it costs nothing. The same additions (of 1024 columns) cost 2.26 us each of VectorE's time from GpSimd, 1.22 on VectorE itself, and none by an accumulating DMA; that one has to be issued ahead by the time it takes to land, here 7.6 and 7.9 us on the median and up to 11.6. And fewer matmuls are a ceiling, not a gain: here 15 us, of which the best arrangement kept 8.

## What was not expected of the hardware

An accumulating DMA from HBM onto SBUF, issued by GpSimd, landed in 7.6 us for 512 KB (median of 20, beside other transfers), cost GpSimd 0.87 us to issue, and left VectorE's splits at 1221 ns. GpSimd's memsets of 1024 columns, 0.96 us each, also left them at 1222. So in these runs it was GpSimd's reads, and neither its writes nor its being busy, that stood against VectorE.
